# Local attention: the value products of two steps issued together in every second step

## The reference

```python
def windowed_attention(q, k, v, k_ctx, v_ctx, sink):
    s_loc = jnp.einsum('bnqkgd,bnjkd->bnkgqj', qb, kb).astype(jnp.float32) * scale
    s_ctx = jnp.einsum('bnqkgd,bjkd->bnkgqj', qb, k_ctx).astype(jnp.float32) * scale
    s_loc = jnp.where(valid[None, :, None, None], s_loc, -jnp.inf)
    p = jax.nn.softmax(jnp.concatenate([sk, s_ctx, s_loc], axis=-1), axis=-1)
    out = (jnp.einsum('bnkgqj,bjkd->bnqkgd', p_ctx, v_ctx)
           + jnp.einsum('bnkgqj,bnjkd->bnqkgd', p_loc, vb))
    return out.reshape(bsz, seq, N_HEADS * hd)
```

## Time and profile before

| what | value |
|---|---|
| median of 3 runs | 2523.92 us (2518.1 to 2526.69) |
| profiled execution | 2527.11 us |
| its span, first to last instruction | 2525.5 us |
| PE busy | 2426.0 us, 96% |
| the local attention, first scores to first matmul of the stage behind it | 1636.4 to 1787.7 us, 151.3 us |
| PE busy in it | 139.7 us |

### The profile page before, as it was taken

One profiled execution on the slowest core, in us unless ns is written; L12 is line 12 of the kernel. 1 busy time (PEld: TensorE's weight loads), 2 busy tenths in 40 slices (PEclk: granted clock), 3 DMA queues, 4 the chain that ended last, 5 costly groups with the idle time before them and its releaser, 6 DMA issues.

```text
span 2525.5 us, 30954 instructions
## 1 busy us (share of the span) xinstructions
PE 2426.0 (96%) x12117; PEld 1992.5 (79%) x12117; DVE 1619.7 (64%) x2045; ACT 1053.8 (42%) x1543; POOL 220.1 (9%) x232
## 2 busy tenths in 40 slices
PE   9999999999999999999999999999995999999996
PEld 7787788888888787787888898766784888888884
DVE  7999733333444564454444963477457999999986
ACT  5234523433331221212113521276253777777765
POOL 1000600000000000000010100000113111111101
PEclk9999899999999999999999999999996999999998
DMA  4111221410021232223222311010237999999987
GB/s 153 67 42 36 81 82 43 167 34 9 34 84 57 78 115 84 100 83 103 88 80 95 142 34 50 34 35 18 85 119 288 349 397 397 392 396 392 396 328 296
DMA packets 116317, 370.27 MB, mean 147 GB/s; under 512 B 6309, under 2 KB 15701, under 8 KB 116208
## 3 DMA queue, kind: packets, MB, share of 16 engines
q1 hardware_dynamic: 94832, 293.63, 30.6%
q0 software_dynamic: 21376, 75.12, 9.5%
HBM read 343.50 MB, written 25.26 MB: 146 GB/s over the span
## 4 chain that ended last, share of the span: by engine, by line
PE 85%; DVE 8%; ACT 3%; DMA 2%; issue 1%; SPq 0%; POOLq 0%; ACTq 0%; DVEq 0%
PE banks L431 24%; PE banks L433 24%; PE banks L432 24%; DVE conv_out L1580 3%; DVE w_lo L425 2%; PE banks L2656 1%; PE banks L540 1%; PE banks L2605 1%; PE banks L2474 1%; PE banks L2453 1%; ACT w_hi L418 1%; PE banks L2625 1%; PE banks L2626 1%; DMA expert_w<-in_w_up 1%; PE banks L2346 1%
## 5 line engine op out<-in xcount | busy, mean ns | idle before, releaser
L2117 DVE TENSOR_TENSOR expert_w_lo<-expert_w,expert_w_hi 128x2048 fp32r<-128x2048 f32 x189 | 426.9, 2286 | 28.1 <-ACT expert_w_hi L1421 26.8
L1421 ACT ACTIVATE expert_w_hi<-expert_w 128x2048 fp32r<-128x2048 f32 x192 | 366.8, 1918 | 150.0 <-PE banks L433 127.8
L431 PE MATMUL banks<-act_hi,w_hi 128*128 128x512 f32 x960 | 375.5, 391 | 3.2 <-DVE w_lo L425 3.0
L433 PE MATMUL banks<-act_hi,w_lo 128*128 128x512 f32 x960 | 373.7, 389 | 0.0
L432 PE MATMUL banks<-act_lo,w_hi 128*128 128x512 f32 x960 | 373.7, 389 | 0.0
L425 DVE TENSOR_TENSOR w_lo<-w_raw,w_hi 128x1024 fp32r<-128x1024 f32 x152 | 186.1, 1250 | 136.3 <-ACT w_hi L418 132.2
L418 ACT ACTIVATE w_hi<-w_raw 128x1024 fp32r<-128x1024 f32 x152 | 157.0, 1058 | 278.0 <-PE banks L433 277.9
L431 PE MATMUL banks<-w_hi,act_hi 128*128 128x512 f32 (+1 forms) x640 | 246.2, 385 | 7.3 <-DVE w_lo L425 3.6
L433 PE MATMUL banks<-w_hi,act_lo 128*128 128x512 f32 (+1 forms) x640 | 243.2, 380 | 0.0
L432 PE MATMUL banks<-w_lo,act_hi 128*128 128x512 f32 (+1 forms) x640 | 242.8, 379 | 0.0
L431 PEld LDWEIGHTS banks<-act_hi,w_hi 128*128 128x128 f32 x960 | 180.2, 188 | 43.1 <-DVE w_lo L425 3.2
(11 more groups left out here) (422 smaller groups left out, 4084.6 us busy)
## 6 DMA issues: line engine op xcount, KB each, us to landing
expert_w<-in_w_gate SPq DMA_DIRECT2D x32, 2048.0 KB, 11.3
expert_w<-in_w_up SPq DMA_DIRECT2D x32, 2048.0 KB, 11.7
expert_w<-in_w_down SPq DMA_DIRECT2D x32, 2048.0 KB, 12.0
ada_w<-in_w_ada POOLq DMA_DIRECT2D x48, 512.0 KB, 4.1
w_raw<-in_mlp_up_w SPq DMA_DIRECT2D x16, 1024.0 KB, 5.4
w_raw<-in_mlp_down_w SPq DMA_DIRECT2D x16, 1024.0 KB, 5.1
w_raw<-in_w_in SPq DMA_DIRECT2D x10, 1024.0 KB, 5.5
w_raw<-in_w_in SPq DMA_DIRECT2D x18, 512.0 KB, 7.7
```

Source lines behind the costliest of these rows:

```text
L431: nc.tensor.matmul(o_, lh, rh, start=start, stop=False)
L433: return nc.tensor.matmul(o_, ll, rh, start=False, stop=stop)
L1421: act.activation(EWH[ring][:, 2 * j:2 * j + 2, :], EW[slot][:, 2 * j:2 * j + 2, :], ACT.Copy).then_inc(w_hi, 1)
L2117: dve.tensor_tensor(EWL[slot][:, c, :], EW[slot][:, c, :], EWH[ring][:, c, :], ALU.subtract).then_inc(w_ready, 1)
```

## The change

Value products are issued in even steps alone. The even step v takes the part that the step before it had as well: with `half` 0 (steps 8, 12, 16, ...) the first 2 key blocks of 4, or the first 3 of 5, and with `half` 1 (steps 10, 14, ...) the last 2. The first part's waits move with it from step 4g+7 to 4g+8. The semaphore that tells DVE and ACT that a group is done is counted in the same step as before (4g+10). No matmul is added or left out, and the order of the key blocks within the sum is the same.

```diff
-                if 7 <= v <= 70:
-                    g, part = (v - 7) // 4, (v - 7) % 4
+                if 7 <= v <= 70 and v % 2 == 0:
+                    g, half = (v - 7) // 4, (v - 7) % 4 // 2
                     t, kv = g // 2, g % 2
-                    if part == 0:
+                    if half == 0:
                         pe.wait_ge(at_c, 4 * g + 4)
                         pe.wait_ge(at_ca, 4 * g + 4)
...
                     keys = [2 + kt for kt in local_tiles(t)] + [0, 1]
-                    more = len(keys) - 4
-                    for n in range(part + more * (part > 0), part + more + 1):
+                    split = len(keys) - 2
+                    for n in range(split * half, split + 2 * half):
                         for par in range(2):
                             m = pe.matmul(BK[6 + t % 2][64 * par:64 * par + 64, 256 * kv:256 * kv + 256],
...
-                    if part == 3:
+                    if half == 1:
                         m.then_inc(at_o, 1)
```

## The result

| | before | after |
|---|---|---|
| median | 2525.32 us (2517.87 to 2530.95, 20 runs) | 2531.53 us (2523.32 to 2538.28, 20 runs) |
| profiled execution, span | 2525.5 us | 2536.4 us |
| its mean granted clock | 0.983 | 0.979 |
| local attention, first scores to the matmuls behind it | 151.3 us | 157.7 us |

The ratio is 1.0025, with a 95% interval of 1.0013 to 1.0036: 6.2 us slower. That is less than the 0.3% the prediction took for its bound, but clear of no change with this many runs, and 2531.53 lies above the forecast range.

The account below looks back on a forecast made before the run. PE, busy 96% of the span, was taken to bound the kernel; middle tiles with their borders +0.3, beginning -0.9 and end +0.1 gave -0.5 us: 2523.4 us against a median of 2523.92, range 2517 to 2530.

Parts of the forecast that it names:

- the switch is all that counts: Faster rival: all merged pairs but two save 0.30 us, borders cost nothing; -9 us, 2514.9 us; chance 0.05.
- Point 2: Five tile borders: two key blocks move from beside PE's wait to behind it, 0.86 us each, +4.3 us.
- Points 3 and 5: Middle tile: border +0.86, three merges -0.90, odd-step wait +0.12, together +0.08 us; end from step 48: +0.1 us.
- Point 4: Attention's beginning, to the border at step 16: -0.74 up to step 8, then less saved through waits; together -0.9 us.
- The third rival: Slower: 2.1 us waits at five borders drop the clock from 2.4 to 1.2 GHz; 9 us, 2532.9 us; chance 0.04.
- The exponentials' chain: Slower rival: late exponentials keep odd steps at 1.99 us, +8.6 us beside the borders' +4.3; 2536.8 us; chance 0.05.
- The floor of point 3: Middle tiles: waiting for ACT's exponential keeps an odd step at 1.37 us or more, not 1.25; costs 0.12 a tile.

## Why the prediction was wrong

- **The bound, and the prices.** PE bounds the attention, and what a group costs held: three merges gave 0.75 where 0.78 was written, two key blocks behind the wait 0.85 to 0.86 where 0.86 was, the border's wait 1.97 where "about 2.1", the middle tile 19.26 where 19.2. The Trainium skill, TensorEngine Tiling (Array Packing), Tiling Modes, says that a change of tiling mode drains TensorE; the runs agree, with about 0.30 us for going in and coming out. The rival "the switch is all that counts" did not come, since it needed PE to have work in the border's wait.
- **Point 2, the borders**: right in mechanism and size, +4.3 forecast; 3.8 without the clock in the run that changes only them, 5 x 0.85 by its tiles.
- **Points 3 and 5, the middle and the end**: +0.08 forecast for a middle tile, 19.26 - 19.15 = 0.11 measured; +0.1 forecast for the end, and from the last border it is 43.46 us against 41.93 with one fall in it, so about nothing.
- **Point 4, the beginning**: -0.9 forecast. The first stretch is 0.80 shorter (forecast 0.74), but the second is 0.57 longer and not 0.15 shorter. Its waits in the changed kernel (who waited for whom, us, times, longest) have two rows that the kernel before does not have there, DVE late for ACT and for PE (that the weight splits on DVE make it late is the prediction's reason, and no run tests it):

```profile
ACT w_probs L1370 <- DVE w_minus_max L1990: 0.8, 2, 0.6
...
PE banks L2610 <- DVE w_probs_T L618: 0.5, 1, 0.5
```

  The term was mis-sized by 0.7 us; without falls the attention is 151.3 instead of the 150.8 that I wrote.
- **The step that failed: the clock stood at nothing in the sum, and its rival at 0.04.** The prediction expected "the clock at 1.00 through the borders", and a fall there was one of its three signs of being wrong; the other two (a wait near 1 us, odd steps above 1.55) did not come. The third rival named the mechanism (the clock falls at the borders' longer waits), its place and a price of 9 us for five falls; the profile shows four falls and 6.4 us, the executions 7 us on the mean. I gave it 0.04, on one row: the wait of 2.3 us near 1786 with the clock at 1.00. That row was one draw. In the eleven profiles of this case this very wait has a fall in nine, and none in the two of the kernel before. The waits of 1.97 us have a fall at 10 of 15 borders (the changed kernel twice, and the run that changes only the borders), those of 1.39 us at none of 5, those of 0.96 us at none of 20. The one row near 1638 that spoke the other way (2.7 us, clock 0.91) should have weighed as much, and in all eleven profiles a fall stands beside that wait. The waits to come were a little shorter than both, and one row for and one against gave no ground for 0.04; the forecast's range had to reach over that case, to 2533.
- **The base.** The result is 8.1 us above the forecast of 2523.4. Of that, 1.4 is the base: three runs gave 2523.92 for the kernel before, twenty gave 2525.32. The rest is the clock and the 0.7 us of point 4, within the spread of the runs. The forecast's own bounds, 2520.9 to 2526.9, are 3 us to each side of 2523.9, not of the 2523.4 that its sum gives; that changes nothing here.
- **The rest.** The exponentials' chain did not take the odd steps. In the changed kernel's timeline of PE an odd step and the even one behind it are

```profile
1702.16 0.55 PE L2605 MATMUL banks<-consts_sb,w_probs_third 128*128 128x128 f32 x3
...
1703.48 0.50 PE L2605 MATMUL banks<-consts_sb,w_probs 128*128 128x128 f32 x3
...
1704.98 1.08 PE L2656 MATMUL banks<-w_probs_T,w_v 128*64 128x256 f32 x8
1705.99 0.55 PE L2605 MATMUL banks<-consts_sb,w_probs 128*128 128x128 f32 x3
```

  1.32 and 2.51 us long: 3.83 for the pair instead of 2 x 1.99, 0.15 less where the forecast had 0.18. The floor of point 3 shows in the scores: they start at 1702.68 and 1704.06, 1.38 apart (floor 1.37), the second 0.05 behind the end of ACT's read of the accumulator (1703.81 + 0.20). The spread of the runs is there ahead of the attention already: in the eleven profiles the first scores start between 1628 and 1641 us though nothing ahead of them differs, and the low clock ahead of them took 1.7 us in the earliest and 13.7 in the latest. The mean granted clock of the 29 executions of before lies between 0.982 and 0.987.

## What to carry to other kernels

Work that stands beside a wait costs nothing, and taking it away gives nothing; put behind the wait, it costs its full length. Look for the waits of the bounding engine first, and move what waits (here four transposes) behind what doesn't, before making the work itself cheaper: that one move took 5.1 us off the attention alone, and 9.6 together with the merges. And price a longer wait of TensorE with the clock in mind: before trusting a row that shows none, look at the same wait in several executions.

## What the runs showed of the hardware

- A switch from 128x128 matmuls to 128x64 column tiles and back costs about 0.30 us: two merges whose step had no other limit gave 0.29 and 0.31. Two whose odd step ran into the wait for ACT's exponential gave 0.16 and 0.14; that makes 0.90 us for 4 merges in a tile.
- A fall of the granted clock from 2.4 to 1.2 GHz at a wait of 1.97 us of PE cost 1.5 to 1.6 us of time, and came at some of the borders of one execution and not at others (four of five, four of five, two of five), at different ones each time. Waits of 1.39 and 0.96 us brought none in 25 borders. Within one execution of the changed kernel the waits and the work around them were the same, and only their moment differed; what decides between two equal waits is not settled here.
- Matmuls whose result is thrown away, put into such a wait, removed the falls at the borders, and the kernel with more work was faster by 0.4 to 0.5% than the one without them (2519.36 us against 2532.06).
